# Value rows first among the projections of block two, three depths of three items computed ahead

## What is computed

```python
proj = hn @ w_in[l]
rq, rk, rv, rg, aq, ak, av, iq, ik, iw = split_columns(proj)
rq = apply_rope(rq...); rk = apply_rope(rk...)
ret_out = retention(rq, rk, rv, rg)
aq, ak, iq, ik = (apply_rope(...) of each)
att_out = dsa_attention(aq, ak, av, iq, ik, iw)   # top 256 keys by indexer score
mixed = jnp.concatenate([ret_out, att_out], axis=-1) @ w_out[l]
```

## Time and profile before

| what | value |
|---|---|
| median of three runs | 2885.61 us (2882.16 to 2888.72) |
| the profiled execution | 2880.87 us, span 2879.1 us |
| PE busy in the span | 2754.2 us (96%) |
| DVE busy in the span | 1789.7 us (62%) |
| PE idle ahead of its first item of `spread_phase` | 7.89 us |
| PE idle ahead of the V items | 8.44 us |

### The profile page before, as it was taken

How to read it: one execution, slowest core, us unless ns; L and a number is a source line. 1 busy time by engine, 2 the same in 40 slices (tenths; PEclk the granted TensorE clock), 3 DMA queues, 4 the chain that set the end, 5 groups by cost and what they waited for, 6 DMA issues and landing times. The chain is left out here.

```text
span 2879.1 us, 38826 instructions
## 1 busy us (share of the span) xinstructions
PE 2754.2 (96%) x13656; PEld 2259.5 (78%) x13656; DVE 1789.7 (62%) x2684; ACT 1246.6 (43%) x2267; POOL 1187.1 (41%) x838
## 2 busy tenths in 40 slices
PE   6999999999999999999998789989999999999998
PEld 6877788887788888888887567867778888887886
DVE  6758757323676666622846888775567778776153
ACT  6226544101533333323544667537553444443243
POOL 2011223334634444544642233531173466665454
PEclk8999999999999999999999899999999999999999
DMA  7431112323421222255530113100242222124452
GB/s 260 156 116 30 30 45 64 106 66 103 139 90 57 87 87 87 73 176 161 186 107 8 37 52 117 52 1 9 81 147 66 81 73 86 67 80 168 150 191 90
DMA packets 176237, 272.35 MB, mean 95 GB/s; under 512 B 13145, under 2 KB 105561, under 8 KB 176089
## 3 DMA queue, kind: packets, MB, share of 16 engines
q1 hardware_dynamic: 176088, 270.39, 28.3%
HBM read 224.21 MB, written 46.14 MB: 94 GB/s over the span
## 5 line engine op out<-in xcount | busy, mean ns | idle before, releaser
L2082 POOL TENSOR_TENSOR sb_out_lo<-sb_out_raw,sb_out_hi 128x512 fp32r<-128x512 f32 (+1 forms) x174 | 312.1, 1801 | 312.7 <-ACT sb_out_hi L2069 312.6
L133 PE MATMUL psum<-sb_out_hi,sb_a_hi 128*128 128x512 f32 x912 | 357.8, 392 | 5.5 <-ACT sb_junk L2293 4.4
L135 PE MATMUL psum<-sb_out_hi,sb_a_lo 128*128 128x512 f32 x912 | 355.1, 389 | 0.0
L134 PE MATMUL psum<-sb_out_lo,sb_a_hi 128*128 128x512 f32 x912 | 355.0, 389 | 0.0
L1555 POOL TENSOR_TENSOR sb_pair_lo<-sb_pair_sum,sb_pair_hi 128x512 fp32r<-128x512 f32 x180 | 236.8, 1327 | 269.6 <-ACT sb_pair_hi L1699 269.6
L133 PE MATMUL psum<-sb_h_hi,sb_w_hi 128*128 128x512 f32 x640 | 256.8, 401 | 2.9 <-DVE sb_h_lo L2229 2.4
L134 PE MATMUL psum<-sb_h_lo,sb_w_hi 128*128 128x512 f32 x640 | 249.6, 390 | 0.0
L135 PE MATMUL psum<-sb_h_hi,sb_w_lo 128*128 128x512 f32 x640 | 249.6, 390 | 0.0
L134 PE MATMUL psum<-sb_h_lo,sb_pair_hi 128*128 128x512 f32 x576 | 224.1, 389 | 0.0
L133 PE MATMUL psum<-sb_h_hi,sb_pair_hi 128*128 128x512 f32 x576 | 224.1, 389 | 0.0
L135 PE MATMUL psum<-sb_h_hi,sb_pair_lo 128*128 128x512 f32 x576 | 224.1, 389 | 0.0
(11 more groups left out here) (488 smaller groups left out, 6370.2 us busy)
## 6 DMA issues: line engine op xcount, KB each, us to landing
act_kept<-sb_gate_up SPq DMA_DIRECT2D x40, 512.0 KB, 2.8
sb_pairs_raw<-in_w_up SPq DMA_DIRECT2D x18, 1024.0 KB, 5.3
sb_late_w<-in_w_ada SPq DMA_DIRECT2D x32, 512.0 KB, 4.9
sb_w_raw<-in_w_in SPq DMA_DIRECT2D x54, 256.0 KB, 3.4
sb_out_raw<-in_w_ffn_down SPq DMA_DIRECT2D x44, 256.0 KB, 3.1
sb_out_raw<-in_w_down SPq DMA_DIRECT2D x44, 256.0 KB, 2.8
sb_act_ring<-act_kept SPq DMA_DIRECT2D x40, 256.0 KB, 4.0
sb_act_late<-act_kept SPq DMA_DIRECT2D x40, 256.0 KB, 4.0
```

Source lines behind the costliest of these rows:

```text
L133: nc.tensor.matmul(out, stationary.hi, moving.hi, start=start, stop=False)
L134: nc.tensor.matmul(out, stationary.hi, moving.lo, start=False, stop=False)
L135: return nc.tensor.matmul(out, stationary.lo, moving.hi, start=False, stop=stop)
L2082: self.nc.gpsimd.tensor_tensor(w.lo, raw, w.hi.bitcast(F32), ALU.subtract).then_inc(self.w_lo, 1)
```

## The change

The order of the groups becomes V, Q, K, G, A. The weights of the first group are now the value columns.

In `scores_phase` SP loads all eight depths of the value weights in two DMAs (three depths, then five) instead of two depths of the query weights; POOL splits three depths instead of two; and PE, behind the last score unit, computes depths 0 to 2 of items 0, 1 and 2. `spread_phase` goes on with depths 3 to 7 of these three items, the raw data being already there.

The search starts at n = 2 instead of n = 1, has two steps at n = 8, and one in each item from n = 9 to 31. `cut_rows` moves behind the copies of items 0 and 1. The transposes of query rows come two items later than the product instead of one. A pair starts with three depths of its first item, asks for its second bank after these (in G still ahead of them), and takes the transposes of the last two query items between its depths. SP issues the second half of a group's weights ahead of the spill of the item before.

```diff
-            sp.dma_start(first_raw[:, :, :], wv[:, 0:2, OFF_RET:OFF_RET + W]).then_inc(first_got, 16)
+            sp.dma_start(first_raw[:, 0:AHEAD, :], wv[:, 0:AHEAD, OFF_RET + 1024:OFF_RET + 1024 + W]).then_inc(first_got, 16)
+            sp.dma_start(first_raw[:, AHEAD:KD, :], wv[:, AHEAD:KD, OFF_RET + 1024:OFF_RET + 1024 + W]).then_inc(later_got, 16)
             sp.wait_ge(rest_got, 16)
+            sp.wait_ge(later_got, 16)
...
+            pe.wait_ge(first_done, 1)
+            pe.wait_ge(dve_read, len(items))
+            for t in range(3):
+                for k in range(AHEAD):
+                    multiply(nc, core.ps[:, t, :], h.tile(k, t), first_w[:, k], k == 0, False)
...
-            split_tile(nc, pool, passed, first_hi, 1, first_raw[:, :, :], first_w[:, :, :], first_done)
+            split_tile(nc, pool, passed, first_hi, 1, first_raw[:, 0:AHEAD, :], first_w[:, :, :], first_done)
...
+AHEAD = 3
...
-Q_, K_, V_, G_, A_ = range(5)
-STEPS = [max(n - 1, 0) for n in range(4 * TB)] + [BITS] * 11
+V_, Q_, K_, G_, A_ = range(5)
+STEPS_IN = [0, 0] + [1] * 6 + [2] + [1] * (3 * TB - 1) + [0] * (TB + 1)
+STEPS = [sum(STEPS_IN[:n]) for n in range(len(STEPS_IN) + 1)]
...
-                weights(0, 2, KD)
                 for n in range(N + 1):
+                    if n < N and items[n][1] == TB - 1 and items[n][0] + 1 < 5:
+                        weights(items[n][0] + 1, 4, KD)
                     if n and items[n - 1][0] in (K_, V_):
...
                     if c + 1 < 5 and t == 0:
                         weights(c + 1, 0, 4)
-                    if c + 1 < 5 and t == TB - 1:
-                        weights(c + 1, 4, KD)
...
-                    if c == Q_ or t > 1 or (c, t) == (A_, 0):
+                    if c == V_ or t > 1 or (c, t) == (A_, 0):
                         bank_free(n)
                     elif t == 0:
                         bank_free(n)
-                        bank_free(n + 1)
+                        if c == G_:
+                            bank_free(n + 1)
...
+                    elif c == V_ and t == 0:
+                        for k in range(AHEAD, KD):
+                            for m in range(3):
+                                steps(m, k, k + 1)
+                    elif t > 1 and (c, t) != (V_, 2):
                         steps(n, 0, KD)
                     elif t == 0:
-                        pair(n, 0, KD)
-                    if n > 1 and items[n - 1][0] == Q_:
-                        turn_free(items[n - 1])
-                        turn_rows(n - 1).then_inc(turned, 1)
+                        steps(n, 0, 3)
+                        bank_free(n + 1)
+                        steps(n + 1, 0, 3)
+                        pair(n, 3, 5)
+                        if c == K_:
+                            turn_free(items[n - 2])
+                            turn_rows(n - 2).then_inc(turned, 1)
+                        pair(n, 5, KD)
+                        if c == K_:
+                            turn_free(items[n - 1])
+                            turn_rows(n - 1).then_inc(turned, 1)
+                    if c == Q_ and t > 1:
+                        turn_free(items[n - 2])
+                        turn_rows(n - 2).then_inc(turned, 1)
...
-                lows(Q_, 2)
+                lows(V_, AHEAD)
+                lows(Q_)
...
-                highs(0, 2, KD)
-                top.cut_rows(act)
+                highs(V_, AHEAD, KD)
...
+                    if n == 2:
+                        top.cut_rows(act)
...
-                    if 0 < n <= N and items[n - 1][0] == Q_:
-                        rows_out(n - 1)
+                    if n > 1 and items[n - 2][0] == Q_:
+                        rows_out(n - 2)
```

More of the change, by code:

```diff
@@ L2493, in scores_phase @@
     small_got, tables_got, rest_got = core.sem("small_got"), core.sem("tables_got"), core.sem("rest_got")
-    first_got, first_hi, first_done, passed = (core.sem(n) for n in ("first_got", "first_hi", "first_done", "passed"))
+    first_got, later_got, first_hi, first_done, passed = (core.sem(n) for n in ("first_got", "later_got", "first_hi", "first_done", "passed"))
     (wi_hi, wi_lo, ws_hi, ws_lo, gemm_done, dve_read, act_read, rr_ready, q_hi, q_lo, turned, turn_hi, keys_out, parts_out_done, s_done, relu_done, added,
@@ L3308, with spread_phase @@
 SUMS_AFTER = {23: 0, 25: 1, 27: 2, 32: 3, 40: 4, 48: 5, 56: 6}
-def spread_phase(core, h, wv, cos, sin, cst, bias, retention_of, spill, q_rows, q_tiles, tops, sparse_of, first_w, next_w, next_raw, next_first):
+def spread_phase(core, h, wv, cos, sin, cst, bias, retention_of, spill, q_rows, q_tiles, tops, sparse_of, first_raw, first_w, next_w, next_raw, next_first):
     nc = core.nc
-    starts = [OFF_RET, OFF_RET + 512, OFF_RET + 1024, OFF_RET + 1536, OFF_AQ]
+    starts = [OFF_RET + 1024, OFF_RET, OFF_RET + 512, OFF_RET + 1536, OFF_AQ]
     items = [(c, t) for c in range(5) for t in range(TB)]
@@ L3348, in spread_phase @@
             rows_no.append(rows_no[-1] + (c != G_))
+        raw_at = lambda n: raw[:, n % 4, :] if n >= KD else first_raw[:, n, :]
         def product(eng, n):
@@ L3363, in row_slot_free @@
             c, t = items[n]
-            if c == Q_:
+            if c == Q_ and t >= 2:
                 eng.wait_ge(turned, place[c, t - 2] + 1)
@@ L3390, in _ @@
                             sp.wait_ge(act_read, t + 1)
-                        sp.dma_start(spill[c - K_][0, t * P:(t + 1) * P, :], rr[:, rows_no[n - 1] % 2, :]).then_inc(spilled[rows_no[n - 1] % 2], 16)
+                        sp.dma_start(spill[c == V_][0, t * P:(t + 1) * P, :], rr[:, rows_no[n - 1] % 2, :]).then_inc(spilled[rows_no[n - 1] % 2], 16)
                     if n == N:
@@ L3394, in _ @@
                     c, t = items[n]
-                    if (c, t) == (V_, 5) or c == G_ and 0 < t < TB - 1:
-                        if c == V_:
+                    if (c, t) == (K_, 5) or c == G_ and 0 < t < TB - 1:
+                        if c == K_:
                             sp.wait_ge(top.masked, TOP_STEPS * len(SUMMED) + 1)
-                        for r in (0, 1) if c == V_ else (t + 1,):
+                        for r in (0, 1) if c == K_ else (t + 1,):
                             ret.load(sp, r, spilled)
@@ L3413, in steps @@
                             pe.wait_ge(lo_done, c * KD + k + 1)
-                        done = multiply(nc, core.ps[:, bank(n), :], h.tile(k, t), first_w[:, k] if c == Q_ and k < 2 else w[:, k], k == 0, k == KD - 1)
+                        done = multiply(nc, core.ps[:, bank(n), :], h.tile(k, t), first_w[:, k] if c == V_ and k < AHEAD else w[:, k], k == 0, k == KD - 1)
                         if t == TB - 1:
@@ L3473, in bank_free @@
                     if n >= 3:
-                        if items[last][0] in (V_, G_):
+                        if items[last][0] == V_:
+                            pe.wait_ge(act_read, last + 1)
+                        elif items[last][0] == G_:
                             pe.wait_ge(act_read, last - 2 * TB + 1)
@@ L3642, in lows @@
                         pool.wait_ge(hi_done, n + 1)
[L3643 to L3647 removed]
+                        nc.gpsimd.tensor_tensor(w.lo[:, k, :], raw_at(n), w.hi[:, k, :].bitcast(F32), ALU.subtract).then_inc(lo_done, 1)
+                pool.sem_inc(hi_done, AHEAD)
+                pool.sem_inc(lo_done, AHEAD)
+                lows(V_, AHEAD)
+                lows(Q_)
                 for c in (Q_, K_):
@@ L3654, in _ @@
                     add_turned(c * TB + TB - 1)
-                lows(G_)
                 for r in range(TB):
@@ L3683, in highs @@
                         n = c * KD + k
-                        act.wait_ge(raw_got[n % 4], 16 * (n // 4 + n % 4 // 2))
                         if c:
+                            act.wait_ge(raw_got[n % 4], 16 * (n // 4 - 1))
                             act.wait_ge(k_used, (c - 1) * KD + k + 1)
-                        nc.scalar.activation(w.hi[:, k, :], raw[:, n % 4, :], ACT.Copy).then_inc(hi_done, 1)
+                        nc.scalar.activation(w.hi[:, k, :], raw_at(n), ACT.Copy).then_inc(hi_done, 1)
                 def turn_done(what):
```

34 lines of the change are left out of this document (12 added, 22 removed).

## The result

The median of the changed kernel is 2891.7 us (2885.88 to 2895.54, 20 runs), that of the kernel before, measured beside it, 2883.5 us (20 runs). The ratio is 1.0025 with a 95% interval of 1.0019 to 1.0031: the change makes the kernel about 8 us slower (5.5 to 9 by the interval). The forecast was 2892. A few executions in the sets of the experiments took over 3100 us, and their medians and ratios leave these out.

The account below looks back on a forecast made before the run. PE is busy 96%, but DVE's chain was taken to decide: G starts 3.6 us later and half clock behind a hole costs 2.7, together +6.3 on the median 2885.6, giving 2892; range 2872 to 2899.

Parts of the forecast that it names:

- Part 1: Loads and split before the barrier: the loads cost nothing; POOL's split, 2.36 us longer, costs DVE 2.0 us.
- Part 2: 27 matmuls moved ahead of the barrier: new phase 2.4 us later, PE's hole 4.0 instead of 7.9, item 3 11 us ahead.
- Part 3: Start of the search: the cut stands behind the copy of item 1, so step 0 begins 5.2 us later.
- Part 4: V items: ACT bounds each step at 4.61 us; with pauses for high parts, the first rope ends at 1679.8.
- Part 5: Q and K items on DVE: low parts add 3.65 us at items 15, 16 and 23; G starts at 1779.1, 3.6 later.
- The hole: PE's wait for DVE ahead of the G items: 11 us, then 6 us at half clock, costing 2.7.
- (a): Rival, low parts at items 15, 16 and 23: POOL and DVE hinder each other less; change -6.7 us, 2879; chance 0.20.
- (b): Rival, items up to G: PE remains the bound and DVE keeps up; G 24.2 us earlier, 2861; chance 0.08.
- (c): Rival, start of the gate stage: PE waits for rope 23, its addition and the key decays; 2897; chance 0.14.
- (d): Rival: moved matmuls bring no more than they cost elsewhere; G starts as before, without the hole; 2886; chance 0.08.

Follow-up runs that it names:

- the late bank: The changed kernel with the cut first, its gate items' pair asking for its second bank only behind four depths of item 24: 2885.5 us, ratio 1.0003.

## Why the prediction was right

**The number.** That 2892 met 2891.7 is in part luck. The forecast added 6.3 us to a median of three runs, 2885.6; twenty runs of the same kernel give 2883.5, so the change itself is 8.2 us in the medians and 7.9 from the mark to the end. The start of the gate items was forecast 3.6 us later and came 4.6 later: the start of the chain was taken 0.45 us too late, its later items 1.4 us too short. What the forecast has right is the mechanism: the later cut, DVE's chain, the hole ahead of the gate items and the clock behind it.

**Part 1.** The step that a longer split costs DVE time was right, its size too large: 1.52 us against 2.0. The split itself took 6.25 us and not 7.08; two POOL operations of half as many columns again do not take half as long again. By the rule of the Trainium skill ("SBUF — State Buffer", section "SBUF: two separate sides"), that the other engine blocks for the whole instruction, DVE would lose all that the split grows by. It grew by 1.53 us and DVE lost 1.52, so here the trace agrees. For the split as a whole it agrees only in part: the 4.7 us of splitting and 1.3 us of another subtraction cost DVE 3.9 us before.

**Part 2.** The barrier came 1.6 us later and not 2.4; PE's hole was 3.7 us against 4.0, the clock behind it 0.50, and the cut, behind the copy of item 1, began 49.8 us behind the mark (forecast 50.1).

**Part 3.** The first compare came at 54.05 against 54.5. That the cut's place was a cost of its own is shown by putting it first: 4.6 us at the gate items, 5.1 in the median.

**Part 4.** Steps of 4.61 us bound by ACT, two pauses for high parts, rope 8 at 100.3 against 100.6.

**Part 5.** Here the prediction took its largest risk, in carrying the 3.65 us of one row over to three items, two of them fp32. They measured 3.8, 3.8 and 4.4. The last is the term that was mis-sized: at item 23 two small operations, `sb_fell` and `sb_cand`, wait as well (1.21 and 1.18 us instead of 0.16), since in the last steps ahead of the gate items they no longer go through PSUM. DVE's rows, then POOL's:

```profile
1773.90 1.21 DVE L2957 TENSOR_TENSOR sb_fell<-sb_cnt,sb_need 128x3 int32<-128x3 f32 x1 [0.21 <-DVE sb_rope_sin L3595]
1775.14 1.18 DVE L2958 SCALAR_TENSOR_TENSOR sb_cand<-sb_fell,sb_later 128x3 int32<-128x3 int32 x1
...
1773.82 1.26 POOL L3656 TENSOR_TENSOR sb_rotated<-sb_rotated,sb_rope_sin 128x512 f32<-128x512 f32 x1 [5.42 <-DVEq L3596]
1775.04 5.62 POOL L3662 TENSOR_TENSOR sb_w_lo<-sb_w_raw,sb_w_hi 128x512 fp32r<-128x512 f32 x4
```

The first of them runs beside POOL's addition, the second beside the first low part. Over the three items the forecast was 1.0 us short. The waits forecast at item 10 (3.4) and item 17 (2.0) are there.

**The hole** was 12.0 us against 11, and its low clock cost 2.5 against 2.7. A hole of the same 12.0 us cost only 1.5 with the cut first, so that this term came out so near is luck. Behind it the gate items gave nothing back.

**Rivals.** (a) fell: low parts cost what the row said, and with a quarter of them the kernel is 13 us faster. (b) fell with the cut first: nothing of PE's was touched. (c) did not occur in the changed kernel, but it stood close behind: the late bank ran into it. (d) fell, since G started 4.6 us later and behind a hole; and the kernels without matmuls ahead were slower: the moved matmuls are worth 3.5 us. The kernel as a whole is slower mainly for two reasons that runs or rows show: the later cut, 4.6 us at the gate items, and the low clock behind the new hole, 2.5 us. With the cut first the gate items start where they did before, so there the 3.5 us just pay for the rest, the longer split (1.5) and the low parts beside fp32 steps with ropes among it; what each of these costs at the gate items no run separates.

## What to carry to other kernels

In this kernel moving work of an engine that is 96% busy gained only as far as another engine's chain started earlier by it: ask which instruction of the chain stands behind the moved work. When a step is put behind another engine's result, as the cut was behind two copies, price what waits for it to the end of the chain. Where POOL has background work beside a DVE chain of short operations, try its instructions in two and four pieces: here POOL got slower and the kernel 4 to 7 us faster. And before a difference of 1 or 2 us between two traces is put down to a change, look at the granted clock behind the holes of both.

## What the runs showed of the hardware that was not expected

**Which small operations wait for POOL.** While POOL subtracts in the changed kernel, an operation on three columns with all its operands in SBUF takes 1.18 to 1.31 us instead of 0.16; the same decision made with one operand in PSUM takes 0.16 to 0.17 at the same time. Ropes, which read PSUM, keep their 0.68 where low parts in two or four pieces run beside them. With POOL's instructions of 128 columns the 1.25 became 0.42, with 256 columns up to 0.70. That fits a wait until the POOL instruction under way ends.

**Longer busy, less in the way.** Sixteen POOL instructions of 128 columns take 8.0 us beside DVE's chain, four of 512 take 5.5, and the chain is shorter beside the sixteen. In the K items the four pieces lose part of this again in item 17; why the G items gain more from four than from two was not settled.

**The same wait, another length of low clock.** The changed kernel and the one with the cut first both wait 12.0 us ahead of the gate items, and later 1.8 and 1.7 us for key rows. Behind both waits the clock differs. Behind the first it is 0.56 in the changed kernel (the row 1785 to 1791 above). Here are the changed kernel at the second wait, the one with the cut first at both, and the kernel before at its own wait of 1.7 us for key rows:

```profile
1802.00:1815.00 13.00, 11.22 (x92) 9.94 (x91) 11.74 (x30) 5.42 (x12) 5.13 (x5) 0.87 0.19 65
...
1779.00:1785.00 6.00, 5.89 (x22) 4.92 (x23) 5.74 (x7) 4.59 (x10) 4.85 (x4) 0.73 0.13 46
1803.00:1809.00 6.00, 5.76 (x60) 5.07 (x62) 5.89 (x14) 2.35 (x5) 2.68 (x3) 1.00 0.22 58
...
1793.50:1799.50 6.00, 4.34 (x17) 3.31 (x17) 4.60 (x10) 4.37 (x10) 4.14 (x5) 0.72 0.25 89
```

From the first key transpose to the first retention output the changed kernel takes 15.9 us and the one with the cut first 14.9; from there to the first transpose of outputs 21.3 and 20.0. So 2.3 us of a difference can hang on stretches of low clock that the kernel's order does not explain. The kernel before has the second stretch too, and 21.2 us there. There is one trace of each kernel, so whether these stretches belong to a kernel or come and go from one execution to the next is open.
